# Second block: the pre norm's factor applied behind the projections, x transposed bank by bank, layers written out

## The reference, cut to what matters

```python
def rms_norm_2(x, g):
    y = x * rsqrt(mean(x * x, axis=-1, keepdims=True) + 1e-6)
    return y * g

for l in range(2):                                   # second block
    h = rms_norm_2(x, pre_norm_g[l])                 # (256, 1024)
    aq, ak, av, ag, bq, bk, bv, bg = split(h @ w_in[l])  # 512 512 512 512 512 128 128 512 columns
    oa = diff_attention(aq, ak, av, lam, rel_bias)   # 4 heads: softmax(q1 k1 + bias) - lam softmax(q2 k2 + bias)
    ya = rms_norm_2(oa, subln_g[l]) * (1 - lam_init) * silu(ag)
    q = rope(rms_norm_2(bq, q_norm_g[l])); k = rope(rms_norm_2(bk, k_norm_g[l]))
    yb = gqa_attention(q, k, bv) * silu(bg)          # 8 query heads of 64 columns, 2 key heads
    y = concatenate([ya, yb]) @ w_out[l]
    x = x + rms_norm_2(y, post_norm_g[l])
```

## Time and profile before

| | |
|---|---|
| runs | 1086.27, 1091.82, 1091.86 us, median 1091.82 |
| the profiled execution | 1091.74 us, of which its span (first to last instruction) is 1090.1 |
| TensorE busy | 1044.1 us, 96% of the span |
| VectorE, ScalarE, GpSimd busy | 765.5, 551.1, 92.7 us |
| mean granted clock of TensorE | 0.976 of full speed |
| the chain that ended last | TensorE 84%, VectorE 5%, issue 5%, DMA 2%, ScalarE 2%, GpSimd 1% |

### The profile page before, as it was taken

One profiled execution on the slowest core, in us unless ns is written; L12 is line 12 of the kernel. 1 busy time (PEld: TensorE's weight loads), 2 busy tenths in 40 slices (PEclk: granted clock), 3 DMA queues, 4 the chain that ended last, 5 costly groups with the idle time before them and its releaser, 6 DMA issues.

```text
span 1090.1 us, 17989 instructions
## 1 busy us (share of the span) xinstructions
PE 1044.1 (96%) x6062; PEld 913.0 (84%) x6062; DVE 765.5 (70%) x1362; ACT 551.1 (51%) x925; POOL 92.7 (9%) x146
## 2 busy tenths in 40 slices
PE   6999999999999999999999999999999979799896
PEld 5887787899998988889999899999978868688675
DVE  5688778897888676777877855465488574586673
ACT  1457745444544457644444444454355564555662
POOL 0041101000000000110000000000011020120100
PEclk9999979999999999999999999999999998899999
DMA  9866745588777558866766465446256510356311
GB/s 369 292 241 212 251 171 209 198 308 294 266 288 270 195 193 307 288 213 214 239 225 221 137 209 197 171 160 212 91 185 230 175 59 21 127 194 210 117 38 49
DMA packets 58080, 219.22 MB, mean 201 GB/s; under 512 B 6532, under 2 KB 12420, under 8 KB 51880
## 3 DMA queue, kind: packets, MB, share of 16 engines
q1 hardware_dynamic: 49232, 170.02, 45.3%
q0 software_dynamic: 5760, 41.95, 10.6%
q10 hardware_dynamic: 3032, 6.57, 1.9%
HBM read 217.46 MB, written 1.06 MB: 200 GB/s over the span
## 4 chain that ended last, share of the span: by engine, by line
PE 84%; DVE 5%; issue 5%; DMA 2%; ACT 2%; POOL 1%; ACTq 0%; DVEq 0%; SPq 0%; POOLq 0%
PE ps L1635 25%; PE ps L1636 24%; PE ps L1637 24%; PE ps L1741 2%; PE ps L1706 1%; PE ps L2111 1%; DMA ada_raw<-in_adastream 1%; PE ps L1686 1%; PE ps L1696 1%; PE ps L2009 1%; DVE w_lo L954 1%; PE ps L1729 1%; DVE h_lo L1033 1%; PE ps L2159 1%; DMA arena<-in_adastream 1%
## 5 line engine op out<-in xcount | busy, mean ns | idle before, releaser
L954 DVE TENSOR_TENSOR w_lo<-raw,w_hi 128x1024 fp32r<-128x1024 f32 (+1 forms) x318 | 359.4, 1171 | 56.8 <-ACT w_hi L539 50.7
L539 ACT ACTIVATE w_hi<-raw 128x1024 fp32r<-128x1024 f32 (+1 forms) x318 | 308.7, 1009 | 126.8 <-DMA raw<-in_wstream 93.0
L1635 PE MATMUL ps<-h_hi,w_hi 128*128 128x256 f32 x704 | 201.2, 286 | 1.4 <-DVE h_lo L1033 1.0
L1637 PE MATMUL ps<-h_hi,w_lo 128*128 128x256 f32 x704 | 199.5, 283 | 0.0
L1636 PE MATMUL ps<-h_lo,w_hi 128*128 128x256 f32 x704 | 199.5, 283 | 0.0
L1635 PE MATMUL ps<-w_hi,h_hi 128*128 128x512 f32 (+1 forms) x480 | 191.7, 399 | 3.9 <-DVE h_lo L1033 3.9
L1636 PE MATMUL ps<-w_lo,h_hi 128*128 128x512 f32 (+1 forms) x480 | 186.6, 389 | 0.0
L1637 PE MATMUL ps<-w_hi,h_lo 128*128 128x512 f32 (+1 forms) x480 | 186.2, 388 | 0.0
L1635 PEld LDWEIGHTS ps<-h_hi,w_hi 128*128 128x128 f32 x704 | 135.1, 192 | 4.7 <-issue 2.4
L1635 PE MATMUL ps<-w_hi,a_hi 128*128 128x512 f32 x352 | 137.5, 391 | 0.7 <-DVE a_lo L1394 0.7
L1636 PE MATMUL ps<-w_lo,a_hi 128*128 128x512 f32 x352 | 137.4, 390 | 0.0
(11 more groups left out here) (208 smaller groups left out, 1349.9 us busy)
## 6 DMA issues: line engine op xcount, KB each, us to landing
raw<-in_wstream SPq DMA_DIRECT2D x296, 512.0 KB, 5.4
ada_raw<-in_adastream POOLq DMA_DIRECT2D x40, 1024.0 KB, 5.1
ada_raw<-in_adastream SPq DMA_DIRECT2D x4, 1024.0 KB, 9.1
arena<-in_adastream SPq DMA_DIRECT2D x4, 1024.0 KB, 10.6
raw<-in_wsmall SPq DMA_DIRECT2D x22, 128.0 KB, 2.1
row<-in_gate_rows ACTq DMA_DIRECT2D x5, 512.0 KB, 3.7
row<-in_params ACTq DMA_DIRECT2D x2, 769.0 KB, 4.6
x<-in_x SPq DMA_DIRECT2D x1, 1024.0 KB, 9.3
```

What stands on the lines that cost most here:

```text
L539: act.activation(w_hi[:, c % SPLIT, at], raw[:, n, 0:width // 2], ACT.Copy)\
L954: nc.vector.tensor_tensor(w_lo[:, c % SPLIT, at], raw[:, (2 * c + h) % RAW, 0:width // 2], w_hi[:, c % SPLIT, at].bitcast(F32), ALU.subtract)\
L1635: nc.tensor.matmul(dst, sh, mh, start=start, stop=False)
L1637: return nc.tensor.matmul(dst, sl, mh, start=False, stop=stop)
```

## The change

- Nothing is multiplied by the pre norm's factor in front of the projections any more. TensorE transposes x itself, as soon as VectorE has added a bank of 512 columns to it (`s_xb`, one count for each of the four banks; the adds come directly behind their multiplications). The squares stand behind the eight copies of step 6 on ScalarE, and write to another place.
- GpSimd computes the factor `rpre` and its half `rpre_half` (one instruction more for each t). They are applied where projections are read: as the scale of ScalarE's copies, squares and tanh, in VectorE's head scaling (`scaled_heads`, which takes the place of `heads`), in the factor of each head's output norm (one GpSimd instruction more, four times a layer) and in the reciprocals of the grouped heads (one VectorE instruction more, eight times a layer).
- The products that nobody reads become none between t = 0 and 1 in the first layer, eight in the second, and four behind the transposes in both; before there were 12 and 2.
- The parameter row is loaded by GpSimd: in the first layer when the last gate has been read (`s_gate`, during the MLP before), in the second when x has been added to. Both layers' gain columns come in one load, long before.
- The loops over the two layers are written out on all engines, with constants in all waits. `s_scores_seen` goes. The three small chunks behind the last layer go, with their loads and splits.

```diff
-WARM_LAYER = (12, 2)
+WARM_LAYER = ((0, 4), (8, 4))
...
-            for k in range(3):
-                load(C_SECOND + DEPTH * C_LAYER + k, wsmall[DEPTH - 1, k], SMALL)
...
-            with pool.Fori(0, DEPTH) as layer, own.loop(layer, DEPTH, 15):
+            for layer in range(DEPTH):
...
+                if layer == 0:
+                    pool.wait_ge(s_gate, 8)
+                else:
+                    pool.wait_ge(s_xb, 4 * layer + 4)
+                pool.dma_start(row[:, 0:R_LEN], params_in[layer:layer + 1, :]
+                               .to_broadcast([P, R_LEN])).then_inc(s_params, 16)
                 for t in range(TT):
                     pool.wait_ge(s_sq, layer * 2 + (8 + t + 1))
-                    rinv(rinv2[:, t:t + 1], mean2[:, t:t + 1], ss2[:, t:t + 1], D, s_rinv)
+                    own.inc(nc.gpsimd.tensor_scalar(mean2[:, t:t + 1], ss2[:, t:t + 1], 1.0 / D,
+                                                    EPS, ALU.mult, ALU.add))
+                    own.wait()
+                    own.inc(nc.gpsimd.tensor_tensor(rpre[:, t:t + 1], mean2[:, t:t + 1],
+                                                    half[:, 0:1], ALU.pow))
+                    own.wait()
+                    nc.gpsimd.tensor_scalar(rpre_half[:, t:t + 1], rpre[:, t:t + 1], 0.5, None,
+                                            ALU.mult).then_inc(s_rinv, 1)
...
-                    rinv(rinv8[:, 0, v], mean8[:, 0, v], ss8[:, 0, v], P, s_yq)
+                    own.inc(nc.gpsimd.tensor_scalar(mean8[:, 0, v], ss8[:, 0, v], 1.0 / P, EPS,
+                                                    ALU.mult, ALU.add))
+                    own.wait()
+                    own.inc(nc.gpsimd.tensor_tensor(mean8[:, 1, v], mean8[:, 0, v],
+                                                    half[:, 0:2], ALU.pow))
+                    own.wait()
+                    nc.gpsimd.tensor_tensor(rinv8[:, 0, v], mean8[:, 1, v], rpre[:],
+                                            ALU.mult).then_inc(s_yq, 1)
...
-            with act.Fori(0, DEPTH) as layer:
+            act.wait_ge(s_pre, 16)
+            for layer in range(DEPTH):
...
-                act.wait_ge(s_f, layer * 4 + 16)
-                act.dma_start(prenorm[:], prenorm_in[bass.ds(layer, 1)]
-                              .rearrange("a p k -> p (a k)")).then_inc(s_pre, 16)
-                squares(4, lambda t: act.wait_ge(s_res, layer * 2 + (6 + t + 1)))
-                act.wait_ge(s_gate, 8)
-                load_row(params_in[bass.ds(layer, 1), :].to_broadcast([P, R_LEN]), R_LEN)
                 lsplit(3, SMALL)
-                act.wait_ge(s_pre, layer * 16 + 16)
...
+                for t in range(TT):
+                    act.wait_ge(s_xb, layer * 4 + 2 * (t + 1))
+                    act.activation(part(t * D, D), x[:, t, :], ACT.Square,
+                                   accum_out=ss2[:, t:t + 1]).then_inc(s_sq, 1)
...
-                    act.activation(bv[:, t, :], ps[:, t, P:2 * P], ACT.Copy, scale=0.5)\
-                        .then_inc(s_cp, 1)
-                    act.activation(sq_b[:, t, 0:P], ps[:, t, 0:P], ACT.Square).then_inc(s_qsq, 1)
+                    act.wait_ge(s_rinv, layer * 2 + (8 + t + 1))
+                    act.activation(bv[:, t, :], ps[:, t, P:2 * P], ACT.Copy,
+                                   scale=rpre_half[:, t:t + 1]).then_inc(s_cp, 1)
+                    act.activation(sq_b[:, t, 0:P], ps[:, t, 0:P], ACT.Square,
+                                   scale=rpre[:, t:t + 1]).then_inc(s_qsq, 1)
...
                 def add(i):
-                    cb, t = (i % 2, i // 2) if by_token else divmod(i, 2)
+                    t, cb = divmod(i, 2)
                     own.wait(marks[i])
                     v = x[:, t, cb * 512:(cb + 1) * 512]
                     ins = nc.vector.tensor_tensor(v, v, y_tmp[:, i, :], ALU.add)
-                    if cb == 1:
+                    if by_bank:
+                        ins.then_inc(s_xb, 1)
+                    elif cb == 1:
                         ins.then_inc(s_res, 1)
                 for i in range(4):
                     dve.wait_ge(*banks_ready[i])
-                    cb, t = (i % 2, i // 2) if by_token else divmod(i, 2)
+                    t, cb = divmod(i, 2)
                     marks.append(own.inc(nc.vector.tensor_tensor(
                         y_tmp[:, i, :], ps[:, cb * 2 + t, :], gate[:, cb * 512:(cb + 1) * 512], ALU.mult)))
-                    if i % 2:
+                    if by_bank:
+                        add(i)
+                    elif cb == 1:
                         add(i - 1)
                         add(i)
+            def scaled_heads(bank, width, token, t_rinv, dst, done):
+                n = width // DH
+                nc.vector.scalar_tensor_tensor(
+                    dst.rearrange("p (h d) -> p h d", d=DH),
+                    bank.rearrange("p (h d) -> p h d", d=DH), token,
+                    t_rinv[:, 0:n].unsqueeze(2).to_broadcast([P, n, DH]), ALU.mult, ALU.mult)\
+                    .then_inc(done, 1)
...
-            with dve.Fori(0, DEPTH) as layer, own.loop(layer, DEPTH, OWN_DVE):
...
-                norm_x(8, layer * 2)
                 lsplit(3, SMALL)
                 operand(16, layer * 4)
                 lsplit(4)
...
-                        heads(ps[:, 2 * j + t, 0:width], width, rinv8[:, t], sq_b[:, t, 0:width],
-                              s_tok)
+                        dve.wait_ge(s_rinv, layer * 2 + (8 + t + 1))
+                        scaled_heads(ps[:, 2 * j + t, 0:width], width, rpre[:, t:t + 1],
+                                     rinv8[:, t], sq_b[:, t, 0:width], s_tok)
...
                         own.inc(nc.vector.reciprocal(recip[:, u], sums[:, u]))
+                        own.wait()
+                        own.inc(nc.vector.tensor_tensor(recip[:, u], recip[:, u], rpre[:],
+                                                        ALU.mult))
...
                         own.wait()
-                        dve.sem_inc(s_scores_seen, 1)
...
+                if layer + 1 < DEPTH:
+                    lsplit(20, SMALL)
+                    lsplit(21, SMALL)
...
-                    marks.append(own.inc(nc.vector.scalar_tensor_tensor(
+                    own.inc(nc.vector.scalar_tensor_tensor(
                         y_tmp[:, i, :], ps[:, cb * 2 + t, :], rinv2[:, t:t + 1],
-                        row[:, R_POST + cb * 512:R_POST + (cb + 1) * 512], ALU.mult, ALU.mult)))
-                    if cb == 1:
-                        for k in range(2):
-                            own.wait(marks[2 * t + k])
-                            v = x[:, t, k * 512:(k + 1) * 512]
-                            last = nc.vector.tensor_tensor(v, v, y_tmp[:, 2 * t + k, :], ALU.add)
-                        last.then_inc(s_res, 1)
-                lsplit(22, SMALL)
+                        row[:, R_POST + cb * 512:R_POST + (cb + 1) * 512], ALU.mult, ALU.mult))
+                    own.wait()
+                    v = x[:, t, cb * 512:(cb + 1) * 512]
+                    nc.vector.tensor_tensor(v, v, y_tmp[:, i, :], ALU.add).then_inc(s_xb, 1)
+                if layer + 1 < DEPTH:
+                    lsplit(22, SMALL)
...
-            with pe.Fori(0, DEPTH) as layer:
-                keep_warm_wide(7, WARM_LAYER[0])
-                transpose_x(4, layer * 4, layer * 2,
-                            between=lambda: keep_warm_wide(2, WARM_LAYER[1]))
+            for layer in range(DEPTH):
+                for t in range(TT):
+                    if t == 1:
+                        keep_warm_wide(0, WARM_LAYER[layer][0])
+                    for pr in range(4):
+                        if pr % 2 == 0:
+                            pe.wait_ge(s_xb, layer * 4 + 2 * t + pr // 2 + 1)
+                        for b in range(2):
+                            k = 2 * pr + b
+                            last = nc.tensor.transpose(
+                                ps[:, 4 + pr, b * S + t * P:b * S + (t + 1) * P],
+                                x[:, t, k * P:(k + 1) * P], ident[:])
+                        if t == 1:
+                            last.then_inc(s_xT, 1)
+                keep_warm_wide(0, WARM_LAYER[layer][1])
```

68 lines of the change are left out of this document (35 added, 33 removed).

## The result

The kernel after took 1077.85 us (median of 4 runs, 1077.06 to 1078.96) beside 1090.76 us for the kernel before (4 runs, 1086.27 to 1091.86) in the same job: ratio 0.989, interval 0.9859 to 0.9921. The forecast was 1085.5 and the range 1081.0 to 1090.0, so the time lies 3.2 us under the range.

What follows compares the result with a forecast made beforehand. TensorE was taken as the bound, busy 96% of the span, with gains only where it idles, near the change at layer entries and attention: 1091.74 - 2.2 - 3.8 - 0.5 + 0.25 = 1085.5 us, range 1081.0 to 1090.0.

Steps and rivals of the forecast that it cites:

- so a difference carries over as it is: Baseline: the profiled execution, 1091.74 us, lies 0.08 us under the median of 1091.82, so savings subtract from it directly.
- First entry, start: Entry of the second block's first layer: TensorE's first useful matmul comes 3.6 us sooner, at 797.6 instead of 801.23.
- Chunk 4: Weights after chunks 0 to 3 become late, limiting gains to 2.2 us (1.1 to 3.6) and 3.8 us (2.6 to 5.7).
- Second entry, start: Entry of the second block's second layer: TensorE could start at 944.1, 5.7 us before 949.79.
- The order m a m a: VectorE's alternating multiply and add loses 0.12 us overlap twice at the second entry and costs 0.25 us at the end.
- Inside the layers: Removed increments save 0.45 us a layer, an extra reciprocal instruction costs 0.2; together -0.25 a layer, -0.5 in all.
- main step: Both entries: TensorE's start moves by 3 us or more and chunk 4 is late; otherwise the forecast is wrong there.
- The sign for the load: Timeline sign at both entries: ScalarE's split of chunk 4 is released by the load of its weights.
- Rival 1: Entries: TensorE's clock falls, chunks 0 to 3 run at half speed, 3.5 us lost together; 1089.0 us, chance 0.15.
- Rival 1's opposite: The stretch at 898.50 loses its clock fall, 3.4 us less; 1082.1 us, chance 0.07.
- rival 2: Chunk 4 at both entries: slow landings give 1087.8 us (chance 0.14), no limit at all 1082.2 us (chance 0.12).
- Rival 3: Written-out loops: fetching new code stalls engines up to 2.7 us each; four stalls give 1096 us, chance 0.06.

Runs made afterwards that it cites:

- e5_mmaa: Kernel after with VectorE's residual order put back to both multiplications, then both adds, as in the kernel before: 1081.85 us, ratio 0.9921 to before.
- b_again: Kernel before, unchanged, run and profiled once more in a later job: 1086.84 us, ratio 0.9989.
- e7_no_warm: Kernel after without the products that nobody reads at the two entries (WARM_LAYER to zeros): 1081.38 us, ratio 0.9932 to before.
- e2_shift: Kernel after with eight more unread products on TensorE before the first projection, at about 40 us: 1081.59 us, ratio 0.9951 to before.
- a_again: Kernel after, unchanged, run and profiled once more in a later job: 1080.31 us, ratio 0.9930 to before.

## Why the prediction was wrong

**The step that failed** is the second paragraph's: "so a difference carries over as it is". The sum was a difference, 6.25 us, and it was subtracted from one execution at 1091.74, which lay 0.08 under a median of three runs. Over 31, 33 and 21 further runs the kernel before has medians of 1087.56, 1087.02 and 1086.87. From these the same sum forecasts 1080.6 to 1081.3, where the kernel after measured 1080.31 and 1079.22. Of the 7.6 us between 1085.5 and 1077.85 the starting point is thus 4.6; another 1.9 are that the first four runs of the kernel after lay under its later medians; 1.1 are that the change gives more than the sum. The first profile of before took 4.5 and 2.6 us more than that of after, at the lower clock, in two stretches of the first attention alone (11.0 - 6.5, 12.7 - 10.1), and I had read such a stretch only in the second block and not asked whether the first block, 73% of the span, carried the same. Three runs of 1086.27, 1091.82 and 1091.86 were a warning of 5.6 us, and my range of 9 us had no term for them.

**The sum itself**, 6.25, was measured as 6.09 on the same two profiles. That is luck, by errors that cancel; at the places that repeat it was too small, with 8.63 measured:

- First entry, start: 3.6 forecast, 3.72 measured. Chunk 4: 2.2 forecast, 3.23 measured. I took a landing of 5.6 us from rows 5; the loads landed in 3.2 at the least, and ScalarE never waited for one. What set it was the squares: I had them ending 7.05 us behind the multiplication (800.6) and the load later, at 7.55, and ScalarE went from them into the split at 6.78; "TensorE stands for 1.4" was 0.36.
- Second entry, start: 5.7 forecast, 5.86 measured. Chunk 4: 3.8 forecast, 4.33 measured, with the load late as forecast for the second half only (0.74) and TensorE standing 1.41 where 1.9 was forecast.
- The order m a m a: a cost of 0.27 forecast at the second entry and of 0.25 at the end. e5_mmaa turned it back and has the first cost as forecast (0.25, inside the entry), but in front of it a gain of 0.53 in the factor that the sum did not have, and at the end a gain of 0.30. Wrong in sign on balance: I counted VectorE's overlap and not what its adds do to GpSimd beside them. The rows were there: the wait of 0.73 for GpSimd's factor stands in rows 4.
- Inside the layers: 0.25 a layer forecast, 0.00 in layer 0, at the same granted 0.96. The increments in the chain gave nothing that can be seen.
- Layer 1: 126.11 to 128.65, a loss of 2.54 that no step had. A layer's inside took 125.9 to 129.1 us over the profiles of before and after (b_again 129.12 for the 126.11), so it is the same luck again, 0.99 of granted clock for 0.96, and this time against the change.

Take only the stretches that repeat, and the change's places sum to 38.53 - 29.90 = 8.6 us, which fits ratios of 0.9930 and 0.9924 (7.6 and 8.3 us of 1087). Against b_again, whose entries met the lower clock, it is 11.6; how often the old first entry does so, three profiles can't tell.

The prediction's own signs of its main step came true: both starts moved by more than 3 us, chunk 4 was late at both, and VectorE's split released it. The sign for the load held only for the second half at the second entry.

**The rivals.** Rival 1, cold first chunks, did not come: the first chunks ran at 1.00 in all three profiles of after. The Trainium skill's rule that I weighed (TensorE: Matmul & The Clock Gate, HAM oscillation — how this bites in real kernels: a wait between bursts can leave the next burst cold) is borne out all the same, by e7_no_warm, where without the fillers the burst behind the wait ran at 0.77 and 0.70, and by b_again; the fillers kept it off. Whether their new places and numbers do it better than the old ones no run shows. Rival 1's opposite, a fall that vanishes (1082.1), was nearest in kind to what happened, but the falls that vanished lay in the first block, and the stretch at 898.50 that it named fell again in the kernel after (888.4 to 895.2 us, at a granted 0.50), whose layer 0 took the same 128.81. Of rival 2's ends, "no limit at all" (3.6) was nearer at the first entry than my own 2.2, and not at the second (5.7 and 3.8 for 4.33); chunk 4 was late at both, as forecast. Rival 3, code that has to be fetched, is dead: with the loops written out no engine shows a new standstill and layer 1's entry is shorter.

**What stays open:** what starts a fall of the clock in a given run. The shift of 3.4 us in the first block (e2_shift) moved the MLP end nowhere outside the range of the others, and the places of its falls differ from the first profile of after no more than those of the unchanged a_again do, which neither shows nor excludes that small shifts decide it. Nor is it shown why the clock rises early in five profiles and not in eight.

## What to carry to other kernels

Before subtracting a forecast from a profiled execution, look at the granted clock of the unchanged part, stretch by stretch, and put the kernel's own spread into the range: here the runs of one kernel in one job lay 6 to 15 us apart, for an effect of 8. Read the price of a moved instruction for the engine beside it too, here for small GpSimd operations beside VectorE adds from SBUF. When a chain is shortened, the weights for the next chunk become late by several things at once; remove them one by one and each looks small, 0.15 and 0.67 us here, together (with a third edit) 1.41.

## What the runs showed of the hardware

GpSimd's small operations on 128 x 1 elements other than the power took 0.19 to 0.20 us with VectorE idle or reading PSUM, 0.41 to 0.60 beside a VectorE add with both operands in SBUF, and 0.62 beside VectorE's scaling of x (943.61 in the kernel before). At the first entry of the kernel after the power on one column, 0.55 us alone, took 1.02 and 1.44 beside VectorE's remainders and splits:

```profile
793.29 1.02 POOL L503 TENSOR_TENSOR rpre<-mean,half 128x1 f32<-128x1 f32 x1
...
794.98 1.44 POOL L503 TENSOR_TENSOR rpre<-mean,half 128x1 f32<-128x1 f32 x1
```

The same code of the first block ended anywhere between 784.37 and 795.67 us, both of these in one job, by how long it ran at a granted clock of 0.5 and whether the clock rose early. A layer's inside took 124.2 us at a granted 1.00 and 128.6 to 129.2 at 0.96.
